# Rooms of the experts in another order, and expert counts summed ahead of the slot positions

## The reference, cut to what matters

```python
lg1 = xt @ w_r1 + b_r1
grp = argmax(lg1); p_grp = softmax(lg1)[grp]
lg2g = (xt @ w_r2 + b_r2).reshape(n, 4, 4)[:, grp]
top_v, top_i = top_k(lg2g, 2); w2 = softmax(top_v)
for e in range(16):
    h = silu(xt @ w_gate[e]) * (xt @ w_up[e])     # 1024 -> 512
    y = y + (h * gates[:, e:e+1]) @ w_down[e]     # 512 -> 1024
```

## Time and profile before

| | |
|---|---|
| median of three runs | 1871.41 us (1868.41 to 1871.54) |
| the profiled execution, its own time | 1867.48 us |
| its span from first to last instruction | 1865.8 us |
| PE busy | 1640.1 us (88% of the span) |
| mean granted clock of PE | 0.938 |
| DMA, all of the span | 437.67 MB, mean 235 GB/s |
| second layer: first load after the ranking | 1529.25 us from the start of the span |
| second layer: end of PE's last tile | 1822.47 us |
| first layer: first load after the ranking | 618.44 us |

### The profile page before, as it was taken

One profiled execution on the slowest core, in us unless ns is written; L12 is line 12 of the kernel. 1 busy time (PEld: TensorE's weight loads), 2 busy tenths in 40 slices (PEclk: granted clock), 3 DMA queues, 4 the chain that ended last, 5 costly groups with the idle time before them and its releaser, 6 DMA issues. The chain is left out here.

```text
span 1865.8 us, 32200 instructions
## 1 busy us (share of the span) xinstructions
PE 1640.1 (88%) x12366; PEld 912.2 (49%) x12366; DVE 549.8 (29%) x1522; ACT 485.3 (26%) x1038; POOL 163.7 (9%) x218
## 2 busy tenths in 40 slices
PE   6999998888897799998599999989888959999990
PEld 3457785665445334332144777666644443443330
DVE  2304636433313300100241155463441151000004
ACT  2112335564501010010110233556633010000102
POOL 1000003200100000000200000131020000000003
PEclk9999999999998799999899999999998959999995
DMA  8421019898760789999652200599987229899974
GB/s 265 155 107 46 24 47 326 300 316 293 244 246 26 261 317 396 398 390 384 248 181 80 72 32 23 179 314 313 321 292 286 77 82 370 327 396 398 384 299 166
DMA packets 204091, 437.67 MB, mean 235 GB/s; under 512 B 22881, under 2 KB 22882, under 8 KB 203938
## 3 DMA queue, kind: packets, MB, share of 16 engines
q1 hardware_dynamic: 187378, 377.25, 56.6%
q0 software_dynamic: 16560, 58.34, 8.3%
HBM read 402.90 MB, written 32.64 MB: 233 GB/s over the span
## 5 line engine op out<-in xcount | busy, mean ns | idle before, releaser
L980 PE MATMUL bank<-wslots,heads 128*32 128x512 f32 (+2 forms) x1152 | 264.5, 634 | 22.7 <-DMA hgrn<-in_w_up 12.4
L680 PE MATMUL bank<-xT,wslots 128*128 128x272 f32 x1024 | 241.8, 393 | 1.5 <-ACT heads L1236 0.8
L680 PEld LDWEIGHTS bank<-xT,wslots 128*128 128x128 f32 x1024 | 191.6, 190 | 40.7 <-issue 3.2
L634 PE MATMUL bank<-wslots,xT 128*128 128x512 f32 x384 | 173.1, 604 | 5.6 <-DMA wslots<-in_w_in 4.0
L731 PE MATMUL bank<-cst,wslots 128*128 128x128 f32 x1024 | 161.7, 286 | 16.4 <-ACT heads L1286 6.2
L980 PEld LDWEIGHTS bank<-wslots,heads 128*32 128x32 f32 (+2 forms) x1152 | 84.8, 133 | 151.3 <-issue 146.7
L1839 DVE TENSOR_TENSOR temps<-temps,bank 128x512 f32<-128x512 f32 x24 | 16.5, 687 | 477.2 <-PE bank L980 477.2
L980 PE MATMUL bank<-hgrn,heads 128*32 128x512 f32 (+2 forms) x640 | 145.1, 600 | 0.0
L731 PEld LDWEIGHTS bank<-cst,wslots 128*128 128x128 f32 x1024 | 114.6, 143 | 44.2 <-issue 35.2
L931 PE MATMUL bank<-wslots,xT 128*128 128x512 f32 x256 | 115.9, 613 | 3.8 <-DVE xT L1601 3.8
L634 PEld LDWEIGHTS bank<-wslots,xT 128*128 128x128 f32 x384 | 72.4, 194 | 93.9 <-issue 89.6
(11 more groups left out here) (317 smaller groups left out, 1965.0 us busy)
## 6 DMA issues: line engine op xcount, KB each, us to landing
wslots<-in_cache_k SPq DMA_DIRECT2D x256, 256.0 KB, 4.6
wslots<-in_cache_v SPq DMA_DIRECT2D x256, 256.0 KB, 4.6
wslots<-in_w_gate SPq DMA_DIRECT2D x22, 2048.0 KB, 17.6
wslots<-in_w_up SPq DMA_DIRECT2D x18, 2048.0 KB, 17.7
wslots<-in_w_down SPq DMA_DIRECT2D x16, 2048.0 KB, 14.2
wslots<-in_w_in SPq DMA_DIRECT2D x14, 2048.0 KB, 10.0
hgrn<-in_w_up SPq DMA_DIRECT2D x10, 2048.0 KB, 20.4
hgrn<-in_w_down SPq DMA_DIRECT2D x10, 2048.0 KB, 15.1
```

The lines of the kernel that those rows point to most:

```text
L634: x = mm(bank[2 + m % 2][:, :], xT[:, c, tok(i)], w[:, c, :], start=(c == 0), stop=(c == DC - 1))
L680: x = mm(bank[6 + g % 2][:, 0:HALF], w[:, c, h * P:(h + 1) * P], xT[:, c, half * HALF:(half + 1) * HALF], start=(c == 0), stop=(c == DC - 1))
L980: x = mm(bank[2 + k][a:z, :], xeT[T_ % 2][:, c, a:z], weights((what, l, e), DC)[:, c, :], start=(c == 0), stop=(c == DC - 1))
```

## The change

The room order becomes `ORDER = (10, 3, 4, 11, 5, 6, 12, 7, 8, 13, 1, 2, 0, 9)`. The rooms have now 96, 96, 64 (four times), 128, 128, 160, 96 rows: the same rooms and the same kinds of tiles, but the single-expert tiles of the 128 and 160 rooms and the tile 32 + 96 stand last (tiles 8 to 11) and not at tiles 2 to 5. Constants that depend on the order follow by themselves. Positions, counts and results do not depend on it.

```diff
-ORDER = (10, 0, 3, 1, 2, 4, 5, 11, 6, 7, 12, 8, 9, 13)
+ORDER = (10, 3, 4, 11, 5, 6, 12, 7, 8, 13, 1, 2, 0, 9)
...
                 pe.wait_ge(msk_ok, l + 1)
+                for j in range(NT):
+                    x = mm(bank[5][:, 0:NE], ones, msk[:, j, :], start=(j == 0), stop=(j == NT - 1))
+                x.then_inc(pos_ps, 1)
                 mm(bank[6][:, 0:NE], con("tri"), msk[:, 0, :], start=True, stop=True)
-                for j in range(NT):
+                for j in range(NT - 1):
...
                 link(V.tensor_tensor(msk[:, :, :], f1, f2, ALU.add), msk_ok)
-                dve.wait_ge(rexp, 2 * l + 4)
-                link(V.tensor_reduce(r1[:, 0], r4[:, 0], AX, ALU.add))
...
-                dve.wait_ge(pos_ps, l + 1)
-
-                cnt = bank[6][:, NT * NE:(NT + 1) * NE]
+                dve.wait_ge(pos_ps, 2 * l + 1)
+                cnt = bank[5][:, 0:NE]
...
                 link(V.tensor_reduce(place_of[:, FIXED:NE, :], rank_tab, AX, ALU.add))
+                dve.wait_ge(pos_ps, 2 * l + 2)
...
                 link(V.tensor_copy(ordi, ordf), order_ok)
+                dve.wait_ge(rexp, 2 * l + 4)
+                link(V.tensor_reduce(r1[:, 0], r4[:, 0], AX, ALU.add))
```

More of the change, by code:

```diff
@@ L411, in build @@
         lg_ps, lg_ok, rexp, msk_ok, pos_ps, order_ok, place_ok, id_ps, id_ok, rk_ok = (
-            sem(x) for x in ("logits_psum", "logits_ready", "route_exps", "masks_ready", "slots_psum", "order_ready", "places_ready", "ids_psum", "ids_ready", "rows_ready"))
+            sem(x) for x in ("logits_psum", "logits_ready", "route_exps", "masks_ready", "counts_then_slots_psum", "order_ready", "places_ready", "ids_psum", "ids_ready", "rows_ready"))
         xe_in = [sem(f"xe_gathered{i}") for i in range(2)]
@@ L1071, in _ @@
                 pe.wait_ge(msk_ok, l + 1)
+                for j in range(NT):
+                    x = mm(bank[5][:, 0:NE], ones, msk[:, j, :], start=(j == 0), stop=(j == NT - 1))
+                x.then_inc(pos_ps, 1)
                 mm(bank[6][:, 0:NE], con("tri"), msk[:, 0, :], start=True, stop=True)
-                for j in range(NT):
-                    later = msk[:, j, :].unsqueeze(1).to_broadcast([P, NT - j, NE])
-                    if j == NT - 1:
+                for j in range(NT - 1):
+                    later = msk[:, j, :].unsqueeze(1).to_broadcast([P, NT - 1 - j, NE])
+                    if j == NT - 2:
                         mm(bank[6][:, NE:NT * NE].rearrange("p (i e) -> p i e", e=NE), con("tri"), msk[:, 1:NT, :],
                            start=False, stop=False)
-                    x = mm(bank[6][:, (j + 1) * NE:(NT + 1) * NE].rearrange("p (i e) -> p i e", e=NE), ones, later,
-                           start=(j == 0), stop=(j == NT - 1))
+                    x = mm(bank[6][:, (j + 1) * NE:NT * NE].rearrange("p (i e) -> p i e", e=NE), ones, later,
+                           start=(j == 0), stop=(j == NT - 2))
                 x.then_inc(pos_ps, 1)
@@ L1684, in route @@
                 link(V.tensor_copy(ordi, ordf), order_ok)
+                dve.wait_ge(rexp, 2 * l + 4)
+                link(V.tensor_reduce(r1[:, 0], r4[:, 0], AX, ALU.add))
+                link(V.tensor_scalar(r1[:, 5], r1[:, 2], 1.0, None, ALU.add))
+                link(V.tensor_tensor(r1[:, 0], r1[:, 0], r1[:, 5], ALU.mult))
+                link(V.reciprocal(r1[:, 6], r1[:, 0]))
+                link(V.tensor_tensor(r1[:, 7], r1[:, 6], r1[:, 2], ALU.mult))
             def extra_plan(l):
-                cnt = bank[6][:, NT * NE:(NT + 1) * NE]
+                cnt = bank[5][:, 0:NE]
                 pos = bank[6][:, 0:NT * NE].rearrange("p (i e) -> p i e", e=NE)
```

## The result

The kernel after takes **1885.01 us** (median of six runs, 1881.92 to 1887.23), the kernel before beside it 1870.82 us (six runs): ratio 1.0069, 95% interval [1.0053, 1.0085]. It is slower by 14.2 us by the medians (12.9 by the ratio) where 6.9 were forecast; the sign and the range were right, the forecast size was half of it.

What follows compares the result with a forecast made beforehand. Late expert weights were taken to bound PE (DMA at 397 GB/s, seven slots). 2 x (4.3 for the order - 0.85 for the counts) = +6.9 us on 1867.48 gives 1874.4; the median stands 3.9 higher: 1878.3 us, range 1866 to 1889.

Steps and rivals of the forecast that it cites:

- What bounds it: Expert stage: PE has the same work in either order, so only the supply of weight loads can change the time.
- The first ten loads: After the ranking, same slots and times as before, landed at 1596.0; tile 2 finds its weights, nothing counted for it.
- The waits: PE waits for weights at tiles 4 and 6, two each per layer, longest some 5 us; none from tile 7 on.
- up10: 26th load, for the last group's up phase at tile 6: lands at 1691.1, making each layer 4.3 us longer.
- is never empty: DMA load queue after the tenth load: always has loads waiting until tile 6's up phase; down7's slot is the tightest.
- The rate: DMA while the groups run: 397 GB/s, the profile's figure for 125 us on end.
- The faster rival: Never-empty queue supplies the groups above the mixed rate, from 420 GB/s; 1864.9 us at 427; chance 0.15.
- The dry queue: Rival: down7's slot comes 12 us later than thought, queue dry for 3.5 us, some 5 us a layer: 1888; chance 0.13.
- My case: Expert stage at 398 GB/s give or take 1.5%, no dry queue: 1874 to 1884 us; chance 0.51.
- No change: Rival: between 404 and 420 GB/s, or one tile's transfers behind up10, the sum is within 3.7 us of nothing; chance 0.21.
- Counts first: Routing: DVE waits 2.41 us where it waited 3.28; gather and all loads come 0.85 us earlier a layer.
- The gate values at the end: Routing: five instructions moved behind the experts' order gain nothing and cost nothing, covered by the first tokens' 6.7 us wait.

Runs made afterwards that it cites:

- the eighth slot: Changed kernel (new room order) with an eighth slot for all down weights, in memory the expert stage doesn't use: 1878.56 us, ratio 1.0039 to the kernel before.

## Why the prediction was right, and where it was half

*What bounds it: right.* Late weights, and nothing else, tell the orders apart: with halved loads both orders take 1839 us.

*The first ten loads: right within 0.8 us.* The tenth landed 67.5 us after the first issue, forecast 66.75. Tile 2's up phase waited 0.44 us where I counted nothing; no half clock came of it.

*The waits: right in place, nearly so in size.* Forecast at tile 4 about 4, and 3 to 5; measured 2.65 and 4.47. At tile 6 2, and 5 (3 to 5 in the working); measured 1.39 and 6.17. None from tile 7 on. Counted from the first load, gate7's wait was to end at 96.45 (1625.7 - 1529.25) and ended at 96.96.

*up10: the step that failed.* It was to land 161.85 us after the first load; its wait ended at 1705.16 - 1539.92 = 165.24, 3.4 later. Behind it the forecast held: 1840.65 - 1705.16 = 135.5 us, forecast 47.1 + 88.6 = 135.7. Of the 3.4, 0.75 is the tenth load. 1.8 is the dry spot (6 x (397 - 278) / 397), and 0.8 that 390 x 97.6 = 38.06 MB were moved and not 37.74. The working said that the queue "is never empty", with down7 the tightest, "some 12 us before it is due to land". Its issue came 128.3 us after the first, where those 12 us put it at 126, since tile 3's down stands behind tile 4's up phase. Of these 2.3 us 1.85 were there when that phase began: up7's wait ended at 1650.12 - 1539.92 = 110.2, forecast 1637.6 - 1529.25 = 108.35. The tenth load is 0.75 of that; the rest arose mainly between gate7 and up7, which took 13.24 us, the time of two loads and a whole tile's store and gather at 397 GB/s, where I had spread the stores evenly over all loads (2 x 5.94 = 11.9). The half clock behind gate7's wait did hide behind up7's, as I had said. But 12 us were no margin. The DMA issues of after from 1666 to 1682 say how long this load took, and those of before from 1599.5 to 1600.5 how long the first load took that was issued after the dry spell, with no load ahead of it:

```profile
wslots<-in_w_down SPq DMA_DIRECT2D x1, 2048.0 KB, 11.2
...
wslots<-in_w_gate SPq DMA_DIRECT2D x1, 2048.0 KB, 11.9
```

12 less 2.3 less 11.2 is below nothing, by 1.5 us: the dry spot, nearly. I had treated "the slot is free before the load is due" as enough, and had left out that a load issued to a queue that is empty or nearly so needed 11 to 12 us here, of which its bytes are 5.3 (2.097 MB at 397 GB/s). With that one load taken off its slot the stage is 297.1 and 297.7 us: the 293.2 + 4.3 = 297.5 of the forecast. The time then is 1880.2, the forecast 1878.3.

*The rate: right.* 397 and 398 GB/s on both sides of the dry spot, as in the earlier trace rows, and 398 over 94.9 us with the eighth slot. The faster rival needed 420 for all of up10's way. For 6 us it can be met (419 from 690 to 696 in after, 423 from 889 to 895 in before), but the fullest 25 us in after's expert stages show 403 (from 804). The Trainium skill (HBM Reference, Specifications) gives about 425 GB/s for a core that streams alone; no run here holds it beside stores and gathers.

*The rivals.* The dry queue, given 0.13, is the mechanism that came true, at its place (tile 3's down, down7), but milder: a slow spot of 6 us worth 1.8, where I had 3.5 of standstill and 1.7 of half clock. It also came sooner: I had asked for a delay of 12 us, and 2.3 were enough. My case and this one together make the result. The span that I gave my case, 1874 to 1884, does not follow from its condition: by the same sum 398 GB/s give or take 1.5% is 1875 to 1881, and 1884 needs 385. "No change" and "faster" fall with the rate.

*Counts first: right.* Here are the first and last rows of it in after:

```profile
1524.51 2.31 PE L1073 MATMUL bank<-smalls,cst 128*128 128x16 f32 x10 [5.95 <-DVE smalls L1642]
...
1526.94 0.17 DVE L1647 SCALAR_TENSOR_TENSOR temps<-bank,cst 128x14 f32<-128x14 f32 x1 [2.48 <-PE bank L1073]
...
1529.53 0.24 DVE L1658 SCALAR_TENSOR_TENSOR temps<-bank,smalls 128x80 f32<-128x80 f32 x1
```

The ranking starts 2.43 us after the first of these matmuls (2.41 forecast; 3.28 before), its end finds the positions ready, and the first load is issued 1539.92 - 1524.51 = 15.41 us after them, against 1529.25 - 1512.99 = 16.26: the 0.85 us forecast. The absolute times named for this (1528.4, 1515.4) were of no use, since everything ahead had shifted by 11.5 us. The gate values at the end cost nothing: they stand behind the ranking, and PE's wait for the first tokens stays.

## What to carry to other kernels

When few buffers stand between a queue and its consumer, write for each load two times: when its slot is freed, plus what a transfer takes from issue to landing in an empty queue, and when it is due; a load that only just makes it by the first will cut the queue. Mix consumers that need much weight per unit of work with ones that need little (groups and single tiles in turn): with the same bytes and slots that was worth 1.2%, and with one more slot 1.6%, while putting either kind in a row lost. And when a change moves the allocation of buffers, look at what the last freed one lets go: a prefetch released by the stage's last phase ran into the store on which everything waits, and cost 4.4 us in a place that nobody had touched.

## What the runs showed of the hardware that I had not expected

A load of 2 MB took 11.9 us to land when no load was ahead of it in its own queue (before, issued at 1599.80), and 11.2 us when the one ahead had almost 3 us to go (down7 in after): over twice what its bytes need at 397 GB/s. A store and a gather were in flight beside either. A store of 512 KB that was issued, by another engine, 0.9 us behind a 2 MB load landed 8.5 us after its issue; with no load in flight beside it, it landed after 3.6. A PE wait of 2.65 us was followed by a phase at a mean granted clock of 0.81, one of 1.39 us by a phase at 1.00.
